# Projection evictions one step forward in the engines' order, and the lambda sums at the start of the mixer stage

## The reference, cut to what matters

```python
for l in range(DEPTH):                                   # DEPTH = 2
    h = _rms_norm(x, norm1_g[l]) * (1.0 + sc1) + sh1     # 256 x 1024
    pa, pb, pc, pd = _split(h @ w_in[l], GROUP_COLS)
    ya = _rwkv7_mixer(pa, ...)                           # scan over time
    yb = _diff_attn_mixer(pb, ...)                       # differential attention
    yc = _spatial_gating_mixer(pc, ...)
    yd = _forgetting_attn_mixer(pd, ...)
    x = x + g1 * (concat(ya, yb, yc, yd) @ w_out[l])
    ...                                                  # conv-GLU feed-forward
```

```python
lam = exp(sum(lam_q1 * lam_k1)) - exp(sum(lam_q2 * lam_k2)) + lambda_init
```

## Time and profile before

| | |
|---|---|
| median of 3 runs | 1676.66 us |
| fastest and slowest of them | 1668.55, 1677.35 us |
| the profiled execution: its time | 1682.92 us |
| its span in the trace | 1681.1 us |
| TensorE busy | 93% of the span |
| VectorE, ScalarE, GpSimd busy | 64%, 53%, 25% |
| mean granted TensorE clock | 0.947 of full speed |

### The profile page before, as it was taken

How to read it: one execution, slowest core, us unless ns; L and a number is a source line. 1 busy time by engine, 2 the same in 40 slices (tenths; PEclk the granted TensorE clock), 3 DMA queues, 4 the chain that set the end, 5 groups by cost and what they waited for, 6 DMA issues and landing times.

```text
span 1681.1 us, 35261 instructions
## 1 busy us (share of the span) xinstructions
PE 1565.3 (93%) x15256; PEld 1418.6 (84%) x15256; DVE 1075.3 (64%) x1790; ACT 890.1 (53%) x1456; POOL 417.9 (25%) x283
## 2 busy tenths in 40 slices
PE   6999998899999878999989898899998989989999
PEld 6898988779998766899878777799987778789987
DVE  3664464456789566677985665666746665676764
ACT  5654563455443554644456565466645654556652
POOL 1342452333443000243421230112211131012220
PEclk8999999999999989999998988899999996999999
DMA  6322211538889341688862302555442410445550
GB/s 249 126 102 78 78 52 42 202 137 337 306 328 353 116 175 46 243 328 315 336 235 100 101 4 76 203 198 176 176 163 76 131 47 28 158 167 176 183 193 26
DMA packets 40043, 275.89 MB, mean 164 GB/s; under 512 B 4560, under 2 KB 4688, under 8 KB 8528
## 3 DMA queue, kind: packets, MB, share of 16 engines
q1 hardware_dynamic: 39888, 273.63, 44.2%
HBM read 272.57 MB, written 1.05 MB: 163 GB/s over the span
## 4 chain that ended last, share of the span: by engine, by line
PE 81%; DVE 8%; ACT 6%; issue 2%; POOL 2%; DMA 1%; SPq 0%; ACTq 0%; POOLq 0%; DVEq 0%
PE ps L547 23%; PE ps L549 22%; PE ps L548 22%; PE ps L555 3%; PE ps L560 2%; ACT wh L527 1%; DVE wl L535 1%; DMA ring<-in_ws 1%; PE ps L2147 1%; DVE x_sb L2960 1%; DVE hTl L687 1%; PE ps L924 1%; PE ps L1045 0%; PE ps L1974 0%; POOL hTl L693 0%
## 5 line engine op out<-in xcount | busy, mean ns | idle before, releaser
L527 ACT ACTIVATE wh<-ring 128x1024 fp32r<-128x1024 f32 (+4 forms) x428 | 437.7, 1028 | 463.6 <-PE ps L549 455.2
L535 DVE TENSOR_TENSOR wl<-ring,wh 128x1024 fp32r<-128x1024 f32 (+3 forms) x364 | 458.4, 1264 | 350.0 <-ACT wh L527 348.8
L547 PE MATMUL ps<-hTh,wh 128*128 128x256 f32 x1904 | 555.0, 292 | 6.0 <-POOL hTl L693 3.7
L549 PE MATMUL ps<-hTh,wl 128*128 128x256 f32 x1904 | 544.1, 286 | 1.6 <-issue 1.6
L548 PE MATMUL ps<-hTl,wh 128*128 128x256 f32 x1904 | 544.8, 286 | 0.0
L547 PEld LDWEIGHTS ps<-hTh,wh 128*128 128x128 f32 x1904 | 366.3, 192 | 15.5 <-issue 13.7
L548 PEld LDWEIGHTS ps<-hTl,wh 128*128 128x128 f32 x1904 | 367.6, 193 | 0.2
L549 PEld LDWEIGHTS ps<-hTh,wl 128*128 128x128 f32 x1904 | 367.5, 193 | 0.0
L543 POOL TENSOR_TENSOR wl<-ring,wh 128x1024 fp32r<-128x1024 f32 x64 | 169.2, 2643 | 627.6 <-ACT wh L527 627.6
L1449 DVE SCALAR_TENSOR_TENSOR arena<-arena 128x1024 f32<-128x1024 f32 x96 | 157.1, 1653 | 0.9 <-DMA arena<-in_ws 0.9
L547 PE MATMUL ps<-wh,acts 128*128 128x512 f32 x366 | 145.2, 397 | 0.8 <-DVE wl L535 0.8
(11 more groups left out here) (465 smaller groups left out, 2180.0 us busy)
## 6 DMA issues: line engine op xcount, KB each, us to landing
ring<-in_ws SPq DMA_DIRECT2D x197, 1024.0 KB, 4.9
arena<-in_ws SPq DMA_DIRECT2D x48, 1024.0 KB, 8.3
ring<-in_ws SPq DMA_DIRECT2D x5, 768.0 KB, 4.4
ring<-in_ws SPq DMA_DIRECT2D x4, 512.0 KB, 3.6
ring<-in_ws SPq DMA_DIRECT2D x2, 780.0 KB, 4.5
rowt<-in_rowp SPq DMA_DIRECT2D x2, 610.0 KB, 3.8
x_sb<-in_x SPq DMA_DIRECT2D x2, 512.0 KB, 3.9
arena<-in_rowp SPq DMA_DIRECT2D x2, 512.0 KB, 4.3
```

The costliest lines, as they stand in the source:

```text
L527: ac.act(unit_hl(u)[0], unit_src(u), ACT.Copy).then_inc(*W.a(("hi", u)))
L535: ve.tt(l, unit_src(u), h, OP.subtract).then_inc(*W.v(("lo", u)))
L547: pe.mm(o_, lh, rh, start=start, stop=False)
L549: return pe.mm(o_, ll, rh, start=False, stop=stop)
```

## The change

Two due times are added to MIXT. The evictions of block b are due at the block's end minus 1.0 instead of plus 0.1. That is the same time as the block's last projection step, so they stand right behind that step in the list and ahead of the splits that belong to the next block's first step. The first piece of df_v gets a name of its own, "dot", and is due at 2.0 in the first part of the stage, between the units of pa; ScalarE's exponentials and GpSimd's tables stay at "lam".

```diff
         def df_v(ve, l):
             S = DF[l]
-            yield "lam"
+            yield "dot"
             ve.wait_ge(*DMA[f"row_l{l}"][0])
...
-        MIXT = dict(rw=3.5, rw_by=1.6, mat_by=1.76, inv_by=1.1, out_by=1.76, df0=17.0, df0_by=0.765, fx0=32.5, fx0_by=0.938, sg=3.8, sg_by=0.618, df1=31.0, df_gap=5.0, df_by=1.1, fx1=47.5, fx_gap=1.5, fx_by=1.0, wof=13.0)
+        MIXT = dict(rw=3.5, rw_by=1.6, mat_by=1.76, inv_by=1.1, out_by=1.76, df0=17.0, df0_by=0.765, fx0=32.5, fx0_by=0.938, sg=3.8, sg_by=0.618, df1=31.0, df_gap=5.0, df_by=1.1, fx1=47.5, fx_gap=1.5, fx_by=1.0, wof=13.0, pjo=-1.0, dot=2.0)
...
-            plan_ += weave((0, 2, of(f"pa{l}", range(7))), (4.1, 4, of(f"pav{l}", range(4))), *([(1.1, 1, of("fin", ["rec", "rstd", ("x", 0), ("x", 1)]))] if l == 0 else []))
             T0 = MIXT
+            plan_ += weave((0, 2, of(f"pa{l}", range(7))), (4.1, 4, of(f"pav{l}", range(4))), (T0["dot"], of(f"df{l}", ["dot"])), *([(1.1, 1, of("fin", ["rec", "rstd", ("x", 0), ("x", 1)]))] if l == 0 else []))
...
-            plan_ += weave((0, pjs), *[(end_of[b] + 0.1, of(f"pjv{l}", [b])) for b in range(5)],
+            plan_ += weave((0, pjs), *[(end_of[b] + T0["pjo"], of(f"pjv{l}", [b])) for b in range(5)],
```

## The result

The changed kernel takes **1670.4 us** (median of 20 runs, 1659.6 to 1679.8), the kernel before in the same comparison 1678.3 (20 runs, 1668.6 to 1683.1). The ratio is **0.9958, with a 95% interval of 0.9941 to 0.9976**: 7.0 us less, between 4.0 and 9.9. That is on the edge of what a measurement of this kernel tells from no change.

The account below looks back on a forecast made before the run. TensorE, busy 93%, bounds the kernel; its 13.6 us of waits for the moved eviction L1927 cap the move's own gain. Per layer -4.8 + 0.3 = -4.5 us, -9.0 for two: 1667.7 us, range 1660 to 1675.

Parts of the forecast that it names:

- rival 1: RWKV's inversion and heads follow the slower VectorE chain, so only 1.6 to 3.5 us a layer gained, about 1671.5; chance 0.22.
- Block 2's eviction: On VectorE, moved right behind the split of block 3's last unit: TensorE starts block 3 4.1 us earlier.
- Block 1's eviction: On ScalarE, ahead of RWKV's exponentials: it stands still about 1.7 us, and block 4's load is issued 1.05 us later.
- Lambda: Sums moved to the stage's start: 1.06 us leave VectorE before block 2's eviction, cancelling the 1.05 us delay; new place costs 0.
- Block 3's eviction: On VectorE, behind the landed load, GpSimd's products and splits: block 4 starts 4.8 us earlier, a gap remaining before it.
- Blocks 0 and 4: Block 0's copies cost 0; block 4's copy on VectorE delays L2816 of RWKV's inversion, +0.3 us a layer.
- Rival 4: Slower: the remaining gap falls before block 4 and its clock stays low; 7.5 us a layer lost, about 1692; chance 0.03.

## Why the prediction was right, and where it wasn't

The number held: 1670.4 against 1667.7 and a range of 1660 to 1675. The class it gave the higher chance, faster by over 0.5%, missed by a little: 0.42%. The mechanism was right in its main lines and one term was sized at twice what it is. That the number held is in part luck. The traces bear out 4.9 of the 9.0 us that the sum had. The range reached to the middle of rival 1, so it would have held that too: 1678.3 less 4.9 is 1673.4. And three of the four signs that I had named for being wrong came: a wait of 4.5 us at block 4 (over 3.6), an inversion (L2816) that starts only 2.4 / 2.2 us earlier (under 3), and VectorE waiting for the parameters' row. The fourth, a slow stretch through block 4, did not.

- **Block 2's eviction.** Predicted: the wait falls from 4.8 to under 1 us, block 3 starts 4.1 earlier. Measured: 1.31 left, 3.4 / 3.2 earlier. The missing 0.7 us is the split ahead of the eviction, late by the 0.7 us that two other splits lost beside GpSimd.
- **Block 1's eviction.** Predicted: ScalarE stands for 1.7 us at L1935 and the load goes out 1.05 later. Measured: 1.73 on ScalarE, as the changed kernel's row shows, and 1.82 at the load.

```profile
924.51 0.39 ACT L1935 ACTIVATE arena<-ps 128x256 f32<-128x256 f32 x1 [1.73 <-PE ps L549]
```

- **Lambda.** Right at block 3 (1.1 us by the evictions-only kernel, 1.06 predicted). ScalarE has no wait for the sums any more. At the new place VectorE did wait for the parameters' row, 0.73 us in layer 0, where the sum had 0.1 at most; the row took 4.4 us to land in place of 3.8:

```profile
889.93 0.19 DVE L2167 TENSOR_TENSOR small<-rowt 128x32 f32<-128x32 f32 x1 [0.73 <-DMA rowt<-in_rowp]
```

  The cover held it: with the sums alone moved the whole time is 0.9999.
- **Block 3's eviction: the step that failed.** "GpSimd's scaling and its first products, which ended at 950.31 + 1.42 = 951.73, 7.0 us after the landing at 944.70. With the landing at 945.75 that is 952.8." Those 7.0 us, and the 3.0 of VectorE behind them, were taken over as fixed. The 1.42 in them had been measured while VectorE was idle for 3.11 us. They are 8.3 and 3.4, and the landing is 0.5 late. Block 4 starts 2.5 / 2.4 us earlier and not 4.8; the slow start of block 4 stayed, which the sum had not counted as gone.
- **Blocks 0 and 4.** +0.3 a layer was too much: from block 4's start to L2816 the trace of after needs 17.89 us (951.98 to 969.87), before it was 17.75 (960.48 to 978.23), so 0.14, and no run has this eviction moved by itself.
- **The rivals.** By size it is rival 1: 1.6 to 3.5 us a layer, 1671.5 in all, against 2.4 to 2.5 and 1670.4. By place it isn't quite: the chain through GpSimd took the gain back in front of block 4, and behind it, up to L2816, only the 0.14 us above was lost. Rival 4, the low clock in block 4, was right in that the remaining gap falls in front of block 4, and wrong in what follows: 0.66 for 5 us, then 1.00.
- **The rest of the difference.** The two layers give 4.9 us, the runs 7.0 with an interval of 4.0 to 9.9. No other cause is needed. The profiled execution after was 12.5 us shorter than the one before; of that 6.0 us were there at block 0's start in layer 0, ahead of every moved eviction, and more came behind block 4 in layer 0, where the granted clock over 970 to 1035 was 0.84 against 0.76. Neither can be put down to the change. From GpSimd's first L693 of the stage to block 0's start it is 25.0 us before and 23.4 after in layer 0, but 23.4 in both kernels in layer 1, so the sums' new place has no part in it. The kernel with the evictions alone has block 4 within 0.2 us of the changed one, yet L2958 comes 163.0 after block 0's start, in the changed kernel 155.9.

The kernel to keep is the one with block 1's eviction at its old place, block 3's further forward and the later transposes: 0.9863 and 0.9872 on two chips, some 22 us less than before, though its ten executions range from 1645.7 to 1669.8.

## What to carry to other kernels

A duration read from a trace holds only for what its neighbours do at that time. When a change lets one engine run earlier, look at which rows on the chain were measured beside an idle VectorE or GpSimd, and take for them the price of the same instruction beside a busy one, if the trace has such a row. Idle time counts as cover only if nothing slows the work that is to be moved into it. And when a wait is taken away, follow the instruction to the next place that was put in the order for the old timing: here the transposes stood where the rotation used to end, and moving the evictions and the transposes paid only together.

## What the runs showed of the hardware

- VectorE and GpSimd slow each other on f32 operations that read SBUF on both sides: GpSimd's pair of 128x256 products takes 1.42 us beside an idle VectorE and 2.69 to 2.86 beside a busy one. Of VectorE's 128x1024 splits in the kernel before, the 257 with GpSimd idle take 1.21 to 1.23 us; beside GpSimd's rotation products a split took 1.22 to 1.27 there and 1.74 to 2.08 in the changed kernel. So the loss falls on one side or on both. A copy out of PSUM that stands beside the pair in the kernel with block 3's eviction further forward keeps its 0.42. Over the 8 products L2234 of both layers the mean is 1.06 us before and 1.40 after.
- The same program, in stretches of the same work, had a granted clock of 0.91 in one execution and 0.60 in the next over 66 to 100 us after block 0's start (layer 0 of the kernel with later transposes). The some 150 us from block 0's start to L2958 then differ by 10 us. A difference of a few microseconds between two profiles of this kernel says nothing unless it is read stage by stage, from a common event; read so, the block starts and ends of the changed kernel repeat within 0.25 us.
